# Alternating a slice's wide and narrow products in the first product of the feed-forward layers

## The reference

```python
def _sq_relu_mlp(h, w1, w2):
    return jnp.square(jax.nn.relu(h @ w1)) @ w2
...
        h = h + mix
        h = h + _sq_relu_mlp(_rmsnorm(h, ff_norm[layer]), ff_w1[layer], ff_w2[layer])
    return _rmsnorm(h, final_norm)
```

## Time and profile before

| | |
|---|---|
| median of 3 runs | 2377.82 us (2377.27 to 2379.55) |
| the profiled execution | 2379.59 us, its span 2377.9 us |
| granted TensorE clock, mean over the span | 0.993 |
| PE busy | 2335.3 us (98%) |
| PEld busy | 1938.6 us (82%) |
| DVE busy | 1462.2 us (61%) |
| ACT busy | 1098.9 us (46%) |
| DMA | 56.1% of 16 engines' span on the one large queue |

### The profile page before, as it was taken

One profiled execution on the slowest core, in us unless ns is written; L12 is line 12 of the kernel. 1 busy time (PEld: TensorE's weight loads), 2 busy tenths in 40 slices (PEclk: granted clock), 3 DMA queues, 4 the chain that ended last, 5 costly groups with the idle time before them and its releaser, 6 DMA issues.

```text
span 2377.9 us, 35697 instructions
## 1 busy us (share of the span) xinstructions
PE 2335.3 (98%) x13810; PEld 1938.6 (82%) x13810; DVE 1462.2 (61%) x1653; ACT 1098.9 (46%) x1405; POOL 228.9 (10%) x184
## 2 busy tenths in 40 slices
PE   7999999999999999999999999999999999999997
PEld 7876777777888888888888888878888888888886
DVE  5556777756566566566566566675665665665664
ACT  5454444434544344344344546664543443443443
POOL 0002115231000010010010001310000000000001
PEclk9999999999999999999999999999999999999999
DMA  7653333334665665666666565556666666656654
GB/s 224 184 153 94 110 97 100 111 113 129 186 185 190 193 186 195 195 177 202 191 181 197 179 201 169 160 184 187 185 190 193 188 192 195 187 192 192 191 190 155
DMA packets 215450, 411.44 MB, mean 173 GB/s; under 512 B 13264, under 2 KB 19792, under 8 KB 215184
## 3 DMA queue, kind: packets, MB, share of 16 engines
q1 hardware_dynamic: 213888, 406.94, 56.1%
q0 software_dynamic: 1424, 2.49, 0.3%
HBM read 407.28 MB, written 2.10 MB: 172 GB/s over the span
## 4 chain that ended last, share of the span: by engine, by line
PE 95%; DVE 2%; ACT 2%; issue 1%; DMA 0%; POOL 0%; SPq 0%; ACTq 0%; DVEq 0%
PE acc_pair L228 20%; PE acc_pair L230 19%; PE acc_pair L229 19%; PE acc_pair L244 10%; PE tp_pair L244 10%; PE tp_pair L246 5%; PE acc_pair L246 5%; PE tp_pair L790 4%; PE acc_pair L790 1%; PE tp_pair L369 1%; DVE w_lo L217 1%; PE tp_pair L1105 1%; PE acc_pair L1605 1%; PE tp_pair L1605 1%; ACT L783 0%
## 5 line engine op out<-in xcount | busy, mean ns | idle before, releaser
L217 DVE TENSOR_TENSOR w_lo<-raw,w_hi 128x1024 fp32r<-128x1024 f32 (+1 forms) x760 | 1011.5, 1336 | 736.3 <-ACT w_hi L212 730.0
L212 ACT ACTIVATE w_hi<-raw 128x1024 fp32r<-128x1024 f32 (+1 forms) x760 | 801.0, 1055 | 898.5 <-PE acc_pair L230 577.1
L244 PE MATMUL acc_pair<-xT_both,w_hi 128*128 128x512 f32 x1024 | 320.3, 394 | 0.0
L244 PE MATMUL tp_pair<-xT_both,w_hi 128*128 128x512 f32 x1024 | 317.2, 391 | 0.0
L228 PE MATMUL acc_pair<-w_hi,xT_both 128*128 128x512 f32 (+1 forms) x736 | 304.7, 414 | 7.3 <-DVE w_lo L217 7.3
L230 PE MATMUL acc_pair<-w_hi,xT_both 128*128 128x512 f32 (+1 forms) x736 | 286.5, 389 | 0.0
L229 PE MATMUL acc_pair<-w_lo,xT_both 128*128 128x512 f32 (+1 forms) x736 | 286.4, 389 | 0.0
L228 PE MATMUL acc_pair<-w_hi,hidA_hi 128*128 128x512 f32 x640 | 250.9, 392 | 0.4 <-DVE w_lo L217 0.4
L228 PE MATMUL acc_pair<-w_hi,hidB_hi 128*128 128x512 f32 x640 | 250.6, 392 | 0.0
L229 PE MATMUL acc_pair<-w_lo,hidA_hi 128*128 128x512 f32 x640 | 250.1, 391 | 0.0
L230 PE MATMUL acc_pair<-w_hi,hidA_lo 128*128 128x512 f32 x640 | 250.0, 391 | 0.0
(11 more groups left out here) (241 smaller groups left out, 2334.0 us busy)
## 6 DMA issues: line engine op xcount, KB each, us to landing
raw<-in_ff_w SPq DMA_DIRECT2D x512, 512.0 KB, 4.1
raw<-in_ev_w_in SPq DMA_DIRECT2D x112, 512.0 KB, 3.7
raw<-in_od_w_in SPq DMA_DIRECT2D x64, 512.0 KB, 4.3
raw<-in_ev_w_out SPq DMA_DIRECT2D x32, 512.0 KB, 3.6
raw<-in_od_w_out SPq DMA_DIRECT2D x32, 512.0 KB, 3.8
raw<-in_ev_w_in SPq DMA_DIRECT2D x8, 288.0 KB, 5.5
x<-in_x_in SPq DMA_DIRECT2D x4, 512.0 KB, 6.2
gate_w<-in_gx_w SPq DMA_DIRECT2D x8, 256.0 KB, 2.8
```

Of the source, the lines that this page charges most:

```text
L212: act.activation(w_hi[:, j % RING, :, 0:wide], raw[:, j % RING, :, 0:wide], ACT.Copy).then_inc(hi_ready, 1)
L217: dve.tensor_tensor(w_lo[:, j % RING, :, 0:wide], raw[:, j % RING, :, 0:wide], w_hi[:, j % RING, :, 0:wide], ALU.subtract).then_inc(lo_rea ...
L244: nc.tensor.matmul(o[:, :], w_hi[:, j % RING, kt % KU, c * P:(c + 1) * P], both, start=(kt == 0), stop=False)
```

## The change

In a turned unit the eight wide matmuls ran first, then the eight narrow ones. Now each wide matmul is followed by the narrow one of the same slice and column block. The same matmuls run on the same operands; the number of weight loads is the same, since each matmul has its own. The wait at the front of the unit and the semaphore raised by its last matmul stay.

```diff
         def multiply_unit_turned(pe, n, j, bank):
 
             pe.wait_ge(lo_ready, 8 * n + j + 1)
-            tiles = [(kt, c, o) for kt in range(KU * j, KU * j + KU) for c, o in enumerate(four(bank))]
-            for kt, c, o in tiles:
+            for kt in range(KU * j, KU * j + KU):
                 both = xT_both[:, kt, :, :].rearrange("p a t -> p (a t)")
-                nc.tensor.matmul(o[:, :], w_hi[:, j % RING, kt % KU, c * P:(c + 1) * P], both, start=(kt == 0), stop=False)
-            for kt, c, o in tiles:
-                last = nc.tensor.matmul(o[:, T:2 * T], w_lo[:, j % RING, kt % KU, c * P:(c + 1) * P], xT_both[:, kt, 0, :],
-                                        start=False, stop=(kt == KT - 1))
+                for c, o in enumerate(four(bank)):
+                    part = slice(c * P, (c + 1) * P)
+                    nc.tensor.matmul(o[:, :], w_hi[:, j % RING, kt % KU, part], both, start=(kt == 0), stop=False)
+                    last = nc.tensor.matmul(o[:, T:2 * T], w_lo[:, j % RING, kt % KU, part], xT_both[:, kt, 0, :],
+                                            start=False, stop=(kt == KT - 1))
             last.then_inc(unit_used, 1)
```

## The result

The changed kernel takes 2381.94 us (median of 20 runs, 2381.01 to 2383.95), the kernel before 2377.61 us (20 runs, 2375.71 to 2379.87): 4.3 us more, a ratio of 1.0019 with a 95% interval of 1.0012 to 1.0026. It is slower, by about what the text ahead set as the edge of "the same".

The account below looks back on a forecast made before the run. TensorE's own time was taken as the bound: 256 turned units going from 2.793 to 2.784 us gain 2.3 us, so 2377.8 - 2.3 = 2375.5 us, with a range of 2364 to 2388.

Parts of the forecast that it names:

- the edge of "the same": Whole kernel: a measurement tells about 0.2%, 4.8 us, from nothing; smaller differences count as the same.
- What bounds the kernel: Whole kernel: TensorE busy for 98% of the span, about 30% of the time in the turned units' matmuls.
- The settled paces: Long streams of one kind: 0.2268 us for a wide matmul, 0.120 us for a narrow one.
- what a steady alternation costs: Turned units: a pair bounded between 0.3468 and 0.349 us, middle 0.348 taken, 2.3 us gained.
- The prediction's own last sign: Turned units: prediction wrong if, for example, a pattern repeats over several pairs and is not between 0.3468 and 0.349.
- The steps don't heal: Turned units: wide matmuls stay dear after one narrow; pair 0.355 or 0.353, 12 or 8 us lost; chance 0.21.
- The narrow ones hide better: Turned units: wide matmul's slack used for the load after next; 13 or 19 us gained; chance 0.20.
- The bank stalls: Turned units: narrow matmul waits on columns just written, 0.16 us each, 330 us lost; chance 0.01.
- the range: Whole kernel's time: from 2364 to 2388 us, about 0.1 of chance left out on each side.
- the rival's price: Turned units, steps that don't heal: 0.353 us a pair, 8 us lost, 2386 us.
- my case: Turned units: a pair of 0.3465 to 0.350 us, kernel 2372.5 to 2379.5 us, chance 0.58.
- my second bound: Turned units: a pair costs the settled sum, 0.3468 us, a unit 2.774, 4.9 us gained.

Follow-up runs that it names:

- e10: Kernel before, with wide and narrow alternating, but each quarter's first four matmuls wide, wide, narrow, narrow; 2384.52 us, ratio 1.0029 to the kernel before.
- e6: Kernel before, with wide and narrow alternating and the low weights' matmul moving 384 columns; span 2494.9 us, one execution.
- e1: Kernel before, with wide and narrow alternating but each narrow matmul trailing by one column block; span 2381.9 us, one execution.
- e5: Kernel before, with the two matmuls alternating and the low weights' one moving all 512 columns; span 2590.0 us, one execution.
- e12: Kernel before, with wide and narrow alternating, but two and two in each quarter's first unit; 2372.45 us, ratio 0.9977 to the kernel before.

## Why the prediction was wrong

- **What bounds the kernel: right.** TensorE's own pace in the turned units is all that moved; the other engines and PE's waits followed within a few us. The settled paces held (0.2268 and 0.120), and so did the unit of before.
- **The step that failed: the bounds of "what a steady alternation costs".** I let a pair lie between 0.3468 and 0.349 and took the middle, 0.348. I had read a step between the kinds as a cost of its own, measured it once at each end of a run of eight, and carried it over. In fact three quarters of the pairs (6 of 8 layer quarters) cost 0.3533, above my upper bound, and one quarter 0.347, below my middle. The mean, 0.3517, is 0.0026 more than the 0.3491 of before, and 2048 pairs make of that the 5.4 us of the traces. The table of run lengths shows the fault: the cost of a to and fro is 6.6, 3, 16, 19 and 18 ns, so the first matmul behind a long run says nothing about short ones. The prediction's own last sign, a pattern over several pairs outside 0.3468 to 0.349, is what came.
- **"The steps don't heal" (0.21) named the right side and, with 0.353, the right price** for most of the stream. Its sum of 8 us was for all 256 units; the two fast quarters kept 2 x 1.6 us off it (90.17 in place of e10's 91.76). Its mechanism, wide matmuls that always pay 0.235 behind a single narrow one, isn't what happens: their lengths rotate through three values (0.231, 0.239 and, in the third pair, 0.234), and the same code runs at the settled sum in the other state.
- **"The narrow ones hide better" (0.20)** did not come: no alternation of 512 and 256 columns settled under 0.3467. Its premise, that what a narrow matmul has on top is a load that doesn't fit, is weakened by e6 and by the wide stream: 384 columns cost more than their settled sum, and 512 columns have the same 0.0133 us on top as 256. The Trainium skill, TensorE: Matmul & The Clock Gate, section LDWEIGHTS, has 107 ns for a load, which 384 columns at 0.160 us would cover; the trace agrees as far as it goes, with loads every 0.120 us.
- **"The bank stalls" (0.01)** fell with e1 and e5.
- **The chances.** I gave 0.35 to faster and 0.23 to slower; the time lies on the side that I held the less likely, 4.3 us more where 2.3 less were forecast. That it lies inside the range is owed to the rival's price, not to my case, and its size is owed to the entries that the kernel happens to have: e12, with another first unit a quarter, gives the 4.9 us of my second bound. A sign of a repeating pattern was there and I averaged it away: in the timeline that the earlier trace rows are from, every fourth matmul of 288 columns is followed after 0.12 to 0.13 us and the other three after 0.13 to 0.14.
- **What stays open** is what the state is. It is shown that it exists, that it lasts through whole quarters, that it differs with the widths and with the matmuls ahead, and that the change between `w_hi` and `w_lo` (e5) and two matmuls in a row into one bank (e1, e5) don't bring the loss. Which part of TensorE holds it (the feed of moving columns, the weight loads or the order between them) no run tells; the records of the loads are 0.19 us long at either pace.

## What to carry to other kernels

The cost of a matmul in a dense stream is a property of the stream, not of the instruction: with equal widths of 512 it was one number here (0.2267 us), with mixed widths it locked into patterns 2% apart, and one measured step doesn't price a pattern. Read the pace over whole repeats, in every place where the code occurs: two places with the same instructions and other paces are the sign of a state. No order was best throughout. With 512 and 256 columns, sixteen of a kind beat eight by 0.1%, and the alternation was the best (2.773 us a unit) or the worst (2.826), by its entry; with 512 and 384, runs of eight lost to the better of the two alternations (3.265 against 3.253). So a mixed order has to be measured in place, with its entry, and a fix by a special first unit is fragile.

## What the runs showed of the hardware that was not expected

- A stream of alternating 512- and 256-column matmuls, at a granted clock of 1.00, goes at 0.3467 or at 0.3533 us a pair; of 512 and 384 at 0.407 or 0.413. In both cases the two paces lie 6.7 ns apart.
- The state lasts: at least 32 units, 90 us, without a change, and it survives the border between groups. Small matmuls in between can turn it: eight did in the first quarter of the changed kernel (slow to fast), four in that of e6 (fast to slow), and neither did in the second layer of e10.
- With 512 and 256 columns, runs of two of a kind cost 3 ns a to and fro, runs of four 16 ns, long runs 18 to 20 ns; with 512 and 384, runs of eight cost 65 ns.
